# Quarter products in the two level recurrences, score products split by queries, and rotations moved among the triangular levels

## What is computed

```python
# block 1, each layer: gated delta rule, 4 heads (the kernel's chunks are tiles of 128 tokens)
a_mat = strict_lower(kbeta @ k.T * decay) + eye
sol = triangular_solve(a_mat, rhs)          # done in the kernel by doubling levels 1, 2, ..., 64
# block 1, each layer: latent attention, 8 heads, 128 plain and 64 rotated features per head
s = (q_nope @ k_nope.T + q_pe @ k_pe.T) * 192 ** -0.5 ; causal softmax ; p @ v
# block 2, layer 0: HGRN recurrence, 6 heads, also done by doubling levels 1 ... 64
# block 2, both layers: memory attention, 4 heads of 64;  layer 1: forgetting attention, 12 heads of 64, causal
s = q @ k.T * 64 ** -0.5 (+ decay)
```

## Time and profile before

| | us |
|---|---|
| median of 3 runs (1657.63 to 1662.73) | 1659.18 |
| the profiled execution, its own time | 1661.63 |
| its span, first to last instruction | 1659.9 |
| PE busy | 1590.7 |
| DVE busy | 1031.9 |
| ACT busy | 894.0 |
| mean granted TensorE clock | 0.985 |

### The profile page before, as it was taken

The page is one execution under the profiler, slowest core; times in us unless marked ns, Lnnn a source line. Parts: engine busy times, 40 slices in busy tenths (PEclk is TensorE's granted clock), DMA queues, the critical chain, the costliest instruction groups (busy, mean ns, idle before and its releaser), DMA issues.

```text
span 1659.9 us, 24422 instructions
## 1 busy us (share of the span) xinstructions
PE 1590.7 (96%) x10098; PEld 1379.4 (83%) x10098; DVE 1031.9 (62%) x1585; ACT 894.0 (54%) x1420; POOL 64.3 (4%) x58
## 2 busy tenths in 40 slices
PE   7999989998998999999999999989999999999999
PEld 7989877998887778889988888879888888678887
DVE  6877674897756655555685654555655555765544
ACT  4986473596555546445536544444554446754442
POOL 0013000011200000000000000000000001000000
PEclk9999999999999999999999999999999999999999
DMA  6634224452412565555422665644565553245652
GB/s 223 190 94 142 77 77 152 141 178 62 150 61 93 191 227 181 190 187 161 151 95 79 206 195 182 191 120 146 180 225 179 178 177 128 77 153 183 197 178 101
DMA packets 205695, 253.06 MB, mean 152 GB/s; under 512 B 19216, under 2 KB 185360, under 8 KB 205456
## 3 DMA queue, kind: packets, MB, share of 16 engines
q1 hardware_dynamic: 205584, 251.50, 47.6%
HBM read 250.43 MB, written 1.05 MB: 152 GB/s over the span
## 4 chain that ended last, share of the span: by engine, by line
PE 78%; DVE 11%; ACT 8%; issue 1%; DMA 1%; SPq 0%; POOL 0%; DVEq 0%; ACTq 0%; POOLq 0%
PE bank L799 76%; ACT arena L1482 4%; DVE weights_rest L2029 3%; DVE arena L2177 2%; ACT weights_high L1482 2%; PE bank L1257 1%; ACT L1477 1%; ACT L1482 1%; DMA ring<-in_w_in 1%; PE bank L856 1%; DVE xT_rest L2422 1%; PE bank L1191 0%; DVE x L2391 0%; PE bank L836 0%; DVE arena L2282 0%
## 5 line engine op out<-in xcount | busy, mean ns | idle before, releaser
L2029 DVE TENSOR_TENSOR weights_rest<-ring,weights_high 128x1024 fp32r<-128x1024 f32 (+3 forms) x414 | 476.4, 1195 | 172.6 <-ACT weights_high L1482 171.0
L1482 ACT ACTIVATE weights_high<-ring 128x1024 fp32r<-128x1024 f32 (+3 forms) x414 | 400.1, 1020 | 133.1 <-PE bank L799 115.2
L799 PE MATMUL bank<-weights_high,xT_high 128*128 128x512 f32 (+2 forms) x880 | 334.3, 384 | 8.8 <-DVE xT_rest L2422 3.5
L799 PE MATMUL bank<-weights_high,xT_rest 128*128 128x512 f32 (+2 forms) x816 | 305.9, 375 | 0.0
L1482 ACT ACTIVATE arena<-bank 128x512 f32<-128x512 f32 (+5 forms) x313 | 142.3, 476 | 284.1 <-PE bank L799 275.7
L799 PE MATMUL bank<-xT_high,weights_high 128*128 128x256 f32 (+1 forms) x944 | 278.8, 295 | 5.2 <-DVE xT_rest L2123 2.5
L799 PE MATMUL bank<-xT_rest,weights_high 128*128 128x256 f32 (+1 forms) x944 | 271.9, 288 | 0.0
L799 PE MATMUL bank<-xT_high,weights_rest 128*128 128x256 f32 (+1 forms) x912 | 262.4, 288 | 0.0
L799 PE MATMUL bank<-weights_rest,xT_high 128*128 128x512 f32 (+2 forms) x696 | 260.5, 378 | 0.0
L799 PEld LDWEIGHTS bank<-weights_high,xT_high 128*128 128x128 f32 x880 | 165.9, 189 | 41.7 <-issue 5.4
L799 PEld LDWEIGHTS bank<-xT_high,weights_high 128*128 128x128 f32 (+1 forms) x944 | 184.5, 195 | 13.1 <-DVE weights_rest L2029 5.3
(11 more groups left out here) (186 smaller groups left out, 1956.6 us busy)
## 6 DMA issues: line engine op xcount, KB each, us to landing
ring<-in_w_in SPq DMA_DIRECT2D x36, 1024.0 KB, 5.3
ring<-in_ffn_w_gate SPq DMA_DIRECT2D x71, 512.0 KB, 4.0
ring<-in_ffn_w_up SPq DMA_DIRECT2D x71, 512.0 KB, 5.0
ring<-in_ffn_w_down SPq DMA_DIRECT2D x34, 1024.0 KB, 4.9
ring<-in_w_out SPq DMA_DIRECT2D x22, 1024.0 KB, 4.9
ring<-in_w_in_a SPq DMA_DIRECT2D x11, 1024.0 KB, 5.3
ring_more<-in_ffn_w_down SPq DMA_DIRECT2D x10, 1024.0 KB, 4.9
ring_more<-in_ffn_w_gate SPq DMA_DIRECT2D x17, 512.0 KB, 4.0
```

The costliest lines, as they stand in the source:

```text
L799: return eng.matmul(o, a, b, start=first, stop=last)
L1482: return eng.activation(dst, src, func, **kw_)
L2029: TTs(rest_slot(b)[:, part], raw_slot(b)[:, part], high_slot(key)[:, part].bitcast(F32), ALU.subtract).then_inc(*dv.mark(("rest", key, z)))
```

## The change

- In `schedule()` the five rotations are spread out: rotation 4 (the keys') goes behind `ukv` 1 1 at level 16, rotation 0 and the projection `mz` 0 between the two halves of level 32, rotation 1 into level 64, and rotations 2 and 3 behind `gdn_o` 0, after the triangular levels. `mz` 0 stood at level 64 before. DVE's part of a rotation now waits for the last product that reads the rounded latents (key `v`, l, 1, 1), and ACT's copy of the first transposed probabilities waits for rotation 3.
- `quarters` gives at level 64 the one 64x64 block that is not zero: for U the lower rows and the upper columns, for D (flip) the reverse. PE, ACT and DVE all work on that block alone.
- Every score product of 64 rows becomes two, for queries 0 to 63 and 64 to 127 of the tile.
- Each HGRN level up to 32 makes the two diagonal 64x64 blocks (24 products in place of 12, 64 columns of weights and 64 moving), and level 64 only the upper right block (12 products). DVE copies them with six predicated copies of 64x256 (three before, 128x512), and at level 64 with three plain copies of 64x256.

```diff
--- before.py
+++ after.py
@@ -167,14 +167,14 @@
         out += [("gdn_a", l, n) for n in range(2)]
         rots = [("rot", l, i) for i in (4, 0, 1, 2, 3)]
         beside = {2: ([("uq", l, 0)], [("uq", l, 1)]), 4: ([("uq", l, 2)], [("uq", l, 3)]),
-                  8: ([("ukv", l, 0, 0)], [("ukv", l, 0, 1)]), 16: ([("ukv", l, 1, 0)], [("ukv", l, 1, 1)]),
-                  32: (rots[0:3], rots[3:5]), 64: ([proj("mz", 0)], [("sc", f"m{l}", 0)])}
+                  8: ([("ukv", l, 0, 0)], [("ukv", l, 0, 1)]), 16: ([("ukv", l, 1, 0)], [("ukv", l, 1, 1), rots[0]]),
+                  32: ([rots[1]], [proj("mz", 0)]), 64: ([rots[2]], [("sc", f"m{l}", 0)])}
         out += [("tri", l, 0, 1), ("trid", l, 0, 1), proj("gz", 1), ("tri", l, 1, 1), ("trid", l, 1, 1)]
         m = f"m{l}"
         for s in LEVELS[1:]:
             for n in range(2):
                 out += [("tri", l, n, s)] + beside[s][n] + [("trid", l, n, s)]
-        out += [("gdn_u", l, 0), ("att", m, 0), ("sm", m, 0), proj("mz", 1), ("gdn_o", l, 0), ("gdn_u", l, 1), ("pt", m, 0)]
+        out += [("gdn_u", l, 0), ("att", m, 0), ("sm", m, 0), proj("mz", 1), ("gdn_o", l, 0), rots[3], rots[4], ("gdn_u", l, 1), ("pt", m, 0)]
         out += [("sc", m, 1), ("gdn_w", l), ("gdn_n", l, 0), ("att", m, 1), ("pv", m, 0), ("gdn_o", l, 1), ("sm", m, 1)]
         out += [proj("mz", 2), ("gdn_n", l, 1), ("parts", f"h{l}", "c", "a")]
         out += [("pt", m, 1), ("att", m, 2), ("pv", m, 1), ("sm", m, 2), ("parts", f"h{l}", ("b", 0)), proj("mz", 3)]
@@ -615,9 +615,12 @@
                 v = v.rearrange(f"p ({' '.join(names)}) -> p {' '.join(names)}", **dict(zip(names[1:], dims[1:])))
             return v
 
-        def quarters(s):
-
-            return [(slice(0, P), slice(0, P))] if s == LEVELS[-1] else [(slice(d, d + 64), slice(d, d + 64)) for d in (0, 64)]
+        def quarters(s, flip=False):
+
+            if s == LEVELS[-1]:
+                lower, upper = slice(64, P), slice(0, 64)
+                return [(upper, lower)] if flip else [(lower, upper)]
+            return [(slice(d, d + 64), slice(d, d + 64)) for d in (0, 64)]
 
         def bcast(ap, n):
             return ap.unsqueeze(2).to_broadcast([ap.shape[0], ap.shape[1], n])
@@ -1003,7 +1006,7 @@
                 for z in range(2) if s < LEVELS[-1] else (1,):
                     b = group(("D", l, n, s, z))
                     for h in range(4):
-                        for at_rows, at_cols in quarters(s):
+                        for at_rows, at_cols in quarters(s, True):
                             o = b[at_rows, h * P:h * P + P][:, at_cols]
                             if z == 0:
                                 ins = mm(o, TT[:, n, 1, h, at_rows], U[:, n, h, at_cols])
@@ -1132,11 +1135,13 @@
                     for f, half in enumerate(halves):
                         o = banks[f][:, c:c + wd]
                         if name[0] == "m":
-                            ins = mm(o, qp[half, hp, tok], qp[half, 4, 0:wd], False, True)
+                            q, k, first, last = qp[half, hp, tok], qp[half, 4, 0:wd], False, True
                         elif name[0] == "e":
-                            ins = mm(o, qm[half, hp, tok], km[half, hp, 0:wd])
+                            q, k, first, last = qm[half, hp, tok], km[half, hp, 0:wd], True, True
                         else:
-                            mm(o, qf[half, hp, tok], kf[half, hp, 0:wd], t == 0, False)
+                            q, k, first, last = qf[half, hp, tok], kf[half, hp, 0:wd], t == 0, False
+                        for d in (0, 64):
+                            ins = mm(o[d:d + 64], q[:, d:d + 64], k, first, last)
                         if t == NT - 1 and name[0] != "x":
                             ins.then_inc(*pe.mark(("sc", name, hp, f)))
 
@@ -1407,7 +1412,12 @@
                     b = group(("hl", s, g))
                     for i in range(4):
                         n, h = divmod(4 * g + i, 6)
-                        ins = mm(b[:, i * P:i * P + P], hk[:, h, n * P:n * P + P], hX[:, h, n * P:n * P + P])
+                        if s == LEVELS[-1]:
+                            ins = mm(b[0:64, i * P + 64:i * P + P], hk[:, h, n * P:n * P + 64], hX[:, h, n * P + 64:n * P + P])
+                            continue
+                        for d in (0, 64):
+                            c = n * P + d
+                            ins = mm(b[d:d + 64, i * P + d:i * P + d + 64], hk[:, h, c:c + 64], hX[:, h, c:c + 64])
                     ins.then_inc(*pe.mark(("hl", s, g)))
 
             def st_hg_o(st):
@@ -1849,6 +1859,8 @@
                     nk = kw(name, t) // P
                     if att_before[name, hp]:
                         ac.wait_ge(*at(("pv", *att_before[name, hp])))
+                    if (name[0], hp) == ("m", 0):
+                        ac.wait_ge(*at(("qp", int(name[1]), 3)))
                     copy(a["pt"][:, t, 0:nk], g, ps(g, nk, 2, P), ("pts", name, hp, t))
 
             def st_ffn(st):
@@ -2322,6 +2334,7 @@
                 _, l, i = st
                 dv.wait_ge(*at(("qr", l, i)))
                 dv.wait_ge(*at(("mn", l)))
+                dv.wait_ge(*at(("v", l, 1, 1)))
                 TTs(qp[:, i, :], qr(i), C("cos"), ALU.mult).then_inc(*dv.mark())
                 dv.wait_ge(*dv.last())
                 g = ("rot", l, i)
@@ -2632,8 +2645,15 @@
                 for g in range(3):
                     gk = ("hl", s, g)
                     dv.wait_ge(*at(gk))
-                    mask = over(C(f"level{s}").bitcast(U32), 4)
-                    eng.copy_predicated(ST[:, 4 * g:4 * g + 4, :], mask, ps(gk, 4, P)).then_inc(*dv.mark(("ST",), frees=gk))
+                    if s == LEVELS[-1]:
+                        eng.tensor_copy(ST[0:64, 4 * g:4 * g + 4, 64:P], ps(gk, 4, P)[0:64, :, 64:P]).then_inc(*dv.mark(("ST",), frees=gk))
+                        dv.wait_ge(*dv.last())
+                        continue
+                    for d in (0, 64):
+                        rows_, cols = slice(d, d + 64), slice(d, d + 64)
+                        mask = over(C(f"level{s}")[rows_, cols].bitcast(U32), 4)
+                        eng.copy_predicated(ST[rows_, 4 * g:4 * g + 4, cols], mask, ps(gk, 4, P)[rows_, :, cols]).then_inc(
+                            *dv.mark(("ST",), frees=gk))
                     dv.wait_ge(*dv.last())
 
             def st_hg_n(st):
```

## The result

The changed kernel takes 1647.39 us (median of 4 runs, 1645.57 to 1649.94) against 1658.88 us before (1657.63 to 1662.73): a ratio of 0.9928, 95% interval 0.9904 to 0.9952. That is 11.5 us less. The forecast was 16.5 less and 1642.5 us; the measured time lies 4.9 us above the forecast and inside the range of 1637 to 1651. The profiled execution went from 1661.6 to 1645.6 us, 16.0 less, which is almost the sum of the prediction. So the two questions are which terms make up the 16.0, and why the median shows 4.5 of it less. Two executions in the slow state are left out of every figure here, one of 8742.84 us (both bank edits) and one of 1969.53 us (changed, less HGRN).

A forecast was written before the change was run, and what follows sets the result against it. TensorE, busy 96% of the span, was taken as the bound. Triangular stages 12.0 + HGRN 4.5 + scores 0 = 16.5 us off 1661.6 gives 1645.1, less the profile's 2.4 us offset about 1642.5 us; 8-in-10 range 1637 to 1651.

The forecast's parts named there:

- Rotations and mz 0 moved: Triangular levels: hole of 2.9 us before level 64 becomes 0.55, saving 2.35 us a layer; 0.2 lost entering and leaving small blocks.
- my 0 for what comes behind: Rotations 2 and 3 behind gdn_o 0: taken as costing 0, up to 1.2 us a layer if the cover is gone.
- The clock behind the hole: Behind the hole before level 64: low-clock losses of 3.0 us (first layer) and 1.7 us (second) taken as gone.
- Level 64 in one quarter: Triangular level 64: 32 records a layer at 0.06 us each instead of 0.108 to 0.116, saving 1.5 us a layer.
- HGRN levels: Block 2: shorter levels save 7.4 us, less 0.75 waiting for POOL's square and 2.2 for VectorE, net 4.5 us.
- 2.2 us given back: HGRN level 64 waits for VectorE's carry of level 32: comes 3.3 us earlier where TensorE alone would come 5.5 earlier.
- Scores in quarters: Attention score products: twice the products stream the same columns; if all four quarters run together nothing changes, so 0 us.
- the lower bound that the narrower weight loads had: Scores: narrower weight loads save at most some 0.05 us for each of 26 groups, 1.3 us.
- A: Scores: column halves of one head run in turn, 10.8 us more, 1653, or 1647 if partial; chance 0.20 (half of it partial).
- B: HGRN stage keeps its length because VectorE sets it (full-price copies, or new 2 us hole lowering the clock): 1647; chance 0.12.
- C: Triangular levels: moved rotations do not close the hole; 2.35 and the clock stay, 1642.7 + 9.4 = 1652; chance 0.06.
- D: Slower: HGRN waits between 816 and 867 keep the clock low, +31.6 us, 1674, if the whole stretch falls; chance 0.04.

The follow-up runs named there:

- both bank edits: Changed kernel with latent attention's pair 2 value products and pair 3 scores held to banks 0 to 3, memory attention's first value product to bank 4: 1643.95 us, ratio 0.9908.
- changed, less HGRN: Changed kernel with the HGRN levels left as before (full 128x128 products, whole copies): 1651.11 us, ratio 0.9950.
- level 64 alone: Kernel before with only level 64 of the triangular systems in one quarter of the array: 1656.35 us, ratio 0.9984.
- HGRN alone: Kernel before with only the HGRN levels in quarters: 1658.38 us, ratio 0.9992.
- scores alone: Kernel before with only the 64-row score products split by queries: 1659.44 us, ratio 1.0005.
- The moves alone: Kernel before with only the new order of rotations and mz 0 and its waits: 1652.77 us, ratio 0.9971.
- The repetition: The changed kernel again, unchanged, timed beside its parts: 1646.86 us, ratio 0.9927 against the kernel before.
- the version with latent banks and copies: Changed kernel with latent attention's two groups held to banks 0 to 3 and three whole 128x512 predicated copies a level: 1643.62 us, ratio 0.9908.

## Why the prediction was right, and what it missed

**Rotations and mz 0 moved**: right in place and size for the stage itself. The hole in front of level 64 is gone in both layers, and ScalarE's copy costs 0.5 us as forecast. With level 64, and the moved rotations done, the first layer stands 3.3 us earlier at full clock at 217 (forecast 2.35 + 1.5 - 0.2 = 3.65); the 4.1 at 226.6 holds the shorter hole of pair 1. But my 0 for what comes behind did not hold: the move shifts the banks, and 2.3 us go into a hole in front of the first output product, so 1.7 are left. In the second layer no such hole appears; the time from 401 to 529 falls by 6.2 us where 3.65 were forecast. That is 3.8 up to 489, 0.8 in the hole of pair 1, and 1.7 because a hole of 2.29 us in front of this layer's first output product (518.74 before) is gone. The prediction had neither. That the two layers add up to 7.9 against 7.3 forecast is luck: one hole came and another went.

**The clock behind the hole** is the step that failed. It gave 4.7 us, taken from two windows of one profiled execution, and the prediction held that the clock is "of the same size in every execution". It is not. Four profiles have the hole in front of level 64 (before, level 64 alone, HGRN alone, scores alone). In the first layer the stretch at the lower level behind it cost 3.4, 1.7, 1.7 and 0 us, in the second 1.7 us each time: 3.4 us together on average, and the window that I priced was the longest. Of scores alone, first layer:

```profile
175.84:182.00 6.16, 6.16 (x52) 6.16 (x53) 5.83 (x12) 2.49 (x3) 0.00 (x0) 1.00 0.01 3
```

And part of it only moves. Behind the next hole, of 2.2 us, the clock fell in the second layer in 8 of the 9 profiles that have the moves and in none of the 4 without; in the first layer in 5 of 9 and in 2 of 4. Each such stretch costs 1.7 us. The moves alone still lose 3.9 us less to the clock over six executions. But the whole change loses 22.9 us on average against 22.3 before, and without the HGRN levels it already loses 21.8; which of the remaining parts gives the rest back is not shown. In the profiled pair the clock's loss differs by 3.4 us (25.6 and 22.2) and in the means by -0.6, so 4.0 of the 16.0 are not in the medians. That is most of the 4.9 us by which the forecast was too low; without the clock's 4.7 the sum would be 11.8, and 12.5 were measured by span x clock.

**Level 64 in one quarter**: the pace is right, 0.066 us a record; by itself it gives 0.8 and 1.2 us at its place where 1.5 a layer were forecast.

**HGRN levels**: the work is right, 4.4 us at full clock between 702 and 901 against 4.5 forecast (5.3 without the other parts), and POOL's wait and the copies' price were right too. What I had put down as 2.2 us given back shows up as new holes of 0.39 and 1.73 us, 2.1 together, though in front of the transposes and not of level 64, where I had it. The 2.10 us before the memory attention's product stood there before (2.15); its cause is the bank, freed by ScalarE's exponentials, as the version with bank 4 shows.

**Scores in quarters**: 0 was taken, the busy time of the two forms fell by 1.1 us (13.8 + 6.9 to 13.3 + 6.3), and at full clock 1.3 us less are measured at the end. That looks like the lower bound that the narrower weight loads had, but it is the hole of 1.52 us hidden by the longer low clock at 1106; no run shows the 0.05 us a group. On time it can't be told from nothing (1.0005). The rule of the Trainium skill (TensorE: Matmul & The Clock Gate, Part 3, "What overlaps and what doesn't") that weight loads overlap only across row groups does not agree with this: two column halves of one head cost no more than one full product.

**Sum.** By its parts at full clock, 11.8 forecast and 12.2 in the profiled pair; the clock 4.7 forecast, 3.4 in the profiled pair from 129.5 us on, and nothing in the mean. The repetition gives 12.1, with 1.5 of it between 247 and 401 us and not behind 901.

**Rivals.** A is refuted. B is half true: a new hole came, 1.73 us in front of the transposes, and a low clock behind the old one of 2.10 us, but the stage got shorter all the same. Alone, the levels gave no time, as B says. C did not happen. D did not happen: its sign, a clock below 1 between 816 and 893, is there (0.69 from 847.00 to 852.50), but no stretch of low clock in the changed kernel's HGRN stage is longer than 3.4 us. The mechanism that decides is the forecast's, its clock term mis-sized.

## What to carry to other kernels

Time lost to a low granted clock belongs to an execution as much as to a kernel: before pricing it, compare the mean granted clock of several executions with that of the profiled one, and give the sum once with the clock and once without. A hole that is closed can hand its low clock to the next one, and a low clock can hide a wait, so look at both together. When the order of work changes and buffers are handed out by age, replay which buffer each later group gets; a hole can appear or vanish 50 us behind the edit. When a stage is shortened on the busiest engine, price the next engine's queue operation by operation up to the first wait, because the waits that open there take part of the gain back (2.8 of 7.4 us here).

## What the hardware showed that was not expected

The same hole does not always bring the clock down. In front of the output product behind the HGRN stage (877.06 in the changed kernel) stands a hole of 2.8 us in all the profiles of the first table. At it or right behind it the granted clock fell in the profiles of HGRN alone (889.1), scores alone (887.5) and the changed kernel less HGRN (878.5), and stayed at 1.00 in the others. The last of these falls as a window:

```profile
878.00:885.00 7.00, 5.54 (x13) 4.42 (x14) 6.71 (x9) 5.08 (x7) 0.00 (x0) 0.54 0.00 0
```

Products in four quarters of the array, two of them in the same rows, stream at the pace of full-width pairs (13.3 / 176 = 0.076 us a record against 13.8 / 88 = 0.157 before), while products that all lie in one half of the columns take 0.064 to 0.066 us (24 records in 1.54 us, the HGRN level 64 of the version with latent banks and copies) where pairs over both halves take 0.032.
